# Conditioning weights on a queue and in slots of their own, summed in four stages

## The reference, cut to what matters

```python
for i in range(DEPTH):
    mp = (silu(c_ctx) @ ada_w[i] + ada_b[i]).reshape(6, D_MODEL)      # for the context tokens
    ms = (silu(c) @ ada_w[i] + ada_b[i]).reshape(-1, 6, 1, D_MODEL)   # for the latent tokens
    hp = xp * (1.0 + mp[1]) + mp[0]
    yp = mixer(hp)
    xp = layer_norm(ALPHA * xp + mp[2] * yp)
    ...                                  # the experts with mp[3], mp[4], mp[5]; ms and xs likewise
```

## Time and profile before

| | |
|---|---|
| median of 3 runs | 1439.43 us (1434.58 to 1440.46) |
| the profiled execution | 1439.15 us, of it 1437.3 in the profile's span |
| busy: TensorE, VectorE, ScalarE, GpSimd | 1223.1, 722.3, 344.1, 163.6 us |
| moved by DMA | 290.2 MB, 202 GB/s on average |
| loads of a column, 80 x 512 KB | median 4.7 us from issue to landing, all on SyncE's queue |
| mean granted clock of TensorE | 0.926 |

### The profile page before, as it was taken

The page is one execution under the profiler, slowest core; times in us unless marked ns, Lnnn a source line. Parts: engine busy times, 40 slices in busy tenths (PEclk is TensorE's granted clock), DMA queues, the critical chain, the costliest instruction groups (busy, mean ns, idle before and its releaser), DMA issues.

```text
span 1437.3 us, 14663 instructions
## 1 busy us (share of the span) xinstructions
PE 1223.1 (85%) x5174; PEld 660.0 (46%) x5174; DVE 722.3 (50%) x1580; ACT 344.1 (24%) x728; POOL 163.6 (11%) x222
## 2 busy tenths in 40 slices
PE   6888796999999778999585999989999968899584
PEld 3544354554466333654232555656666423644221
DVE  0598435442312499551013376468886887541114
ACT  1321231222310100311013332234554200311112
POOL 5000310000000000010401401013232000001201
PEclk9999897999999979899798999999999979899797
DMA  9445100327343399189946332234425879199944
GB/s 375 175 162 177 61 1 17 115 105 260 136 167 124 142 335 370 46 356 423 421 204 212 132 125 76 90 112 147 147 85 190 293 275 396 57 400 423 420 169 155
DMA packets 75844, 290.17 MB, mean 202 GB/s; under 512 B 7692, under 2 KB 18188, under 8 KB 61436
## 3 DMA queue, kind: packets, MB, share of 16 engines
q1 hardware_dynamic: 53904, 236.21, 43.3%
q10 hardware_dynamic: 17468, 37.67, 7.4%
q0 software_dynamic: 4400, 15.35, 2.9%
HBM read 261.30 MB, written 27.90 MB: 201 GB/s over the span
## 4 chain that ended last, share of the span: by engine, by line
PE 59%; DVE 13%; DMA 12%; issue 10%; ACT 4%; SPq 1%; ACTq 0%; POOL 0%; POOLq 0%; DVEq 0%
PE bank L580 16%; PE bank L738 7%; PE bank L600 7%; DMA arena<-in_moe_gu 4%; PE bank L947 4%; PE bank L1134 3%; PE bank L758 3%; DVE hT L1884 3%; DVE arena L1908 3%; DMA ring<-in_b_w_out 2%; DMA ring<-in_a_w_down 2%; DVE arena L1884 2%; DVE arena L2460 2%; PE bank L838 2%; PE bank L880 1%
## 5 line engine op out<-in xcount | busy, mean ns | idle before, releaser
L580 PE MATMUL bank<-hT,ring 128*128 128x384 f32 x896 | 304.3, 500 | 18.8 <-DMA ring<-in_a_w_in 14.6
L580 PEld LDWEIGHTS bank<-hT,ring 128*128 128x128 f32 x896 | 173.1, 196 | 142.4 <-issue 19.0
L600 PE MATMUL bank<-ring,arena 128*128 128x512 f32 (+1 forms) x512 | 182.9, 623 | 46.0 <-DMA ring<-in_b_w_out 22.1
L1884 DVE SCALAR_TENSOR_TENSOR hT<-ring,hT 128x1024 f32<-128x1024 f32 x120 | 146.9, 1224 | 9.3 <-DMA ring<-in_ada_wT 5.5
L600 PEld LDWEIGHTS bank<-ring,arena 128*128 128x128 f32 (+1 forms) x512 | 73.5, 198 | 145.9 <-issue 90.9
L738 PE MATMUL bank<-arena,hT 128*64 128x512 f32 x416 | 107.1, 635 | 34.0 <-DMA arena<-in_moe_gu 22.6
L1908 DVE SCALAR_TENSOR_TENSOR arena<-arena,par 128x388 f32<-128x388 f32 x160 | 99.8, 624 | 5.7
L1134 PE MATMUL bank<-hT,ring 128*128 128x384 f32 x256 | 97.6, 507 | 0.2 <-ACT arena L1513 0.2
L738 PEld LDWEIGHTS bank<-arena,hT 128*64 128x64 f32 x416 | 37.5, 146 | 92.1 <-issue 86.4
L2276 DVE TENSOR_TENSOR arena<-arena,bank 128x256 f32<-128x256 f32 x16 | 6.7, 421 | 127.0 <-ACT arena L1635 127.0
L1448 POOL TENSOR_TENSOR arena<-arena 128x192 f32<-128x192 f32 x64 | 43.3, 707 | 214.9 <-PE bank L1167 156.4
(11 more groups left out here) (416 smaller groups left out, 1617.5 us busy)
## 6 DMA issues: line engine op xcount, KB each, us to landing
arena<-in_moe_gu SPq DMA_DIRECT2D x56, 1024.0 KB, 13.3
ring<-in_ada_wT SPq DMA_DIRECT2D x80, 512.0 KB, 4.7
arena<-in_moe_dn SPq DMA_DIRECT2D x28, 1024.0 KB, 19.6
ring<-in_b_w_in SPq DMA_DIRECT2D x40, 512.0 KB, 3.6
ring<-in_a_w_in SPq DMA_DIRECT2D x32, 512.0 KB, 3.5
ring<-in_moe_gu SPq DMA_DIRECT2D x12, 1024.0 KB, 14.2
arena<-acs_rows ACTq DMA_DIRECT2D x32, 384.0 KB, 3.6
yg<-arena ACTq DMA_DIRECT2D x18, 512.0 KB, 7.9
```

Source lines behind the costliest of these rows:

```text
L580: last = mm(keys[j][1][:, 0:T], w[:, k, P * j:P * j + P], hT[:, 4 * half + k, :], start=half == 0 and k == 0, stop=half == 1 and k == 3, s ...
L600: last = mm(keys[t][1][p:p + tokens.shape[1], :], tokens, w[:, j, :], start=k == 0, stop=k == KE - 1, skip_group_check=True)
L1884: ins = ve.scalar_tensor_tensor(out=products, in0=slot(at), scalar=1.0, in1=rows[:, v, :], op0=ALU.mult, op1=ALU.mult, accum_out=mod[:, l, ...
```

## The change

The columns leave `slabs` and the ring. GpSimd issues them on its own queue, in a new function `columns(place)`: it loads the c rows, then the columns one by one into three slots, each as soon as the sum of the column three before is done. Slots, c rows and products lie in parts of the arena that are free in that stage: for places 0 and 1 all six pieces of 1024 together, for 2 and 3 two slots in the scan's old output and one slot and the c rows in `hT`. There are four places with 12, 20, 24 and 24 columns:

- place 0: 12 columns in the first input projection, one after each convolution c = 1 to 12;
- place 1, new: 20 columns in the z projection, two after each gated chunk c = 0 to 9; GpSimd first waits for the end of the scan and of its state outputs;
- place 2: 24 columns in the down projection, where there were 28; GpSimd waits for the last turned-back chunk;
- place 3: 24 columns in the out projection, six between the diagonals and 18 after `rms`; GpSimd waits for its own last products and for the end of the z projection.

SyncE no longer waits for the c rows, nor for sums behind the columns; new is a wait at layer 0's seventh expert slab for 32 sums, since its place overlaps place 1.

```diff
+        c_rows = [v3(a, 2) for a in (free(q_at, 2 * D), free(far_at + 4 * D, 2 * D), hT_free[:, 0:2 * D], hT_free[:, 0:2 * D])]
+        c_slots = [[free(o + D * i) for i in range(3)] for o in (q_at + 3 * D, far_at)]
+        c_slots += [[free(gone_at), free(gone_at + D), hT_free[:, 2 * D:3 * D]]] * 2
+        COLUMNS = (12, 20, 24, 24)
...
         for i in range(2 * KD):
             add("xu", a_in, i // 2, (i % 2,))
-            if i == 1:
-                c_rows_at.append(len(slabs))
-            if i in (1, 2, 4, 5, 7, 8, 10, 11, 13, 14):
-                add_columns(2)
...
                 slabs.append(("down", a_dn[s // 4, 2 * (s % 4) + kp]))
-                if s < 6:
-                    add_columns(4 if (s, kp) in ((1, 0), (2, 1)) else 2)
...
             slabs.append(("out", b_dn[s // 8, s % 8]))
-            if s < 12:
-                add_columns(4 if s in (1, 3, 5, 7) else 2)
...
+                elif l == 0 and m == 6:
+                    sp.wait_ge(sem("summed"), sum(COLUMNS[0:2]))
...
             pool.wait_ge(sem("small_in"), SMALL)
+            def columns(place):
+
+                first = sum(COLUMNS[0:place])
+                pool.wait_ge(sem("small_in"), SMALL + 16 * place)
+                pool.dma_start(c_rows[place].rearrange("p v k -> p (v k)"),
+                               i_["c_rows"].to_broadcast([P, 2 * D])).then_inc(sem("small_in"), 16)
+                for i in range(first, first + COLUMNS[place]):
+                    _, l, j = column_of[i]
+                    if i >= 3:
+                        pool.wait_ge(sem("summed"), i - 2)
+                    pool.dma_start(c_slots[place][i % 3], i_["ada_wT"][l, j]).then_inc(column_landed(i)[0], 16)
+
+            columns(0)
...
+            pool.wait_ge(filled, group["scan_done", 0])
+            for s in range(2):
+                pool.wait_ge(sem(f"out{s}"), 16 * OUT_C)
+            columns(1)
+            pool.wait_ge(filled, group["hn", KE - 1][1])
+            columns(2)
             moe(0)
...
+            pool.wait_ge(sem("xdt_ready"), 2 * KE)
+            pool.wait_ge(sem("wx_ready"), 2 * G)
+            pool.wait_ge(filled, group["in", 3 * KE - 1][1])
+            columns(3)
             moe(1)
...
-                if c in (1, 2, 4, 5, 7, 8, 10, 11, 13, 14):
-                    summed(0, 2)
-            biased(0, 16, 36)
+                if 1 <= c < 13:
+                    summed(0, 1)
+            biased(0, 16, 28)
...
                 ve.tensor_tensor(out=xc, in0=xc, in1=a_sz[:, c, :], op=ALU.mult).then_inc(sem("gA_ready"), 1)
+                if c < 10:
+                    summed(1, 2)
+            biased(0, 28, 48)
...
             diagonals(0)
-            summed(1, 28)
+            summed(2, 24)
...
-            summed(2, 8)
-            biased(1, 16, 24)
...
             diagonals(2, (0, 1))
-            summed(2, 6)
+            summed(3, 6)
             diagonals(2, (2, 3))
...
-            summed(2, 18)
+            summed(3, 18)
             biased(1, 24, 48)
```

67 lines of the change are left out of this document (27 added, 40 removed).

## The result

The changed kernel takes 1429.75 us (median of 20 runs, 1424.68 to 1434.62) against 1438.62 (1431.42 to 1443.68) for the kernel before: a ratio of 0.9941, 95% interval 0.9924 to 0.9957. So it is faster by 8.9 us, where 38.7 were forecast and 1387 to 1424 was the range. The profiled execution has a span of 1431.3 us for 1437.3. Its lines are those of the changed kernel: the sum is L1895, the end of a bias L1904, a convolution's first step L1916, the gating L2084, a projection into the mixer L570, a projection back L590.

The account below looks back on a forecast made before the run. The prediction took the in-order six-slot ring, blocked by columns awaiting VectorE's sums, and waits for VectorE itself as the bound, seldom bandwidth. 23.9 - 2 + 12.8 + 4.0 = 38.7 us off 1439.15 gave 1400, range 1387 to 1424.

Parts of the forecast that it names:

- The first projection: First input projection: fewer columns shorten VectorE's stage by 26.9 us, the start costs 3 (bounds 0 and 6); net 23.9.
- a first k copy later than 132: End of the first input projection: sign that its term is wrong; VectorE's first k copy was expected near 129.
- The z projection: Layer 0: twenty columns come here, VectorE falls back some 7 us and TensorE stalls for banks; 2 us lost.
- The down projection: Layer 0's projection back: 24 columns instead of 28 and a free ring; gain 12.8 us, bounds 16.2 and -23.
- under half of what the engines move: Down projection: SyncE's 2 MB of slabs per 10.4 us until about 532, used to choose a 6 us landing.
- L: Time from a column's issue to landing: 6 then 4.3 us taken in the down projection, 8 in the out projection.
- T: Period per column with three slots, (L + 2.53 + 0.1) / 3: 2.85 us in the down projection, 3.5 in the out.
- The out projection: Layer 1's projection back: 24 columns instead of 32, 18 after the restart as before; gain 4.0 us, bounds 9.2 and -19.
- They move along with the gain: After the projections: the experts' own loads start when routing is planned, so they shift with the gain; 0 us.
- Rival (2): Columns somewhat late throughout, in z, down and out projections; total gain 21.1 us, 1418 us; chance 0.18.
- Rival (3): Three slots cannot cover the queue's latency in the three late stages; slower, 1456 or 1485 us; chance 0.07.
- Rival (4): Projections stay blocked, TensorE now waiting for VectorE through ScalarE's evictions; 1430 to 1440 us; chance 0.04.

Follow-up runs that it names:

- late_start: Changed kernel, but GpSimd's queue issues the c rows and first three columns only once the last ada_w slab has landed; 1422.27 us, 0.9878 of the kernel before.
- z_spread: Changed kernel, with the z projection's 20 columns summed two behind each of the first four chunks, one behind the other twelve; 1432.51 us, 0.9969 of the kernel before.
- experts_held: Changed kernel, with expert slabs moved behind both back projections' slabs and held until the layer's last column sum; 1408.48 us, 0.9791 of the kernel before.
- experts_after: Changed kernel, with expert slabs issued behind the last slabs of the two back projections instead of between them; 1433.65 us, 0.9966 of the kernel before.
- sums_tuned: Changed kernel plus late_start, silu_last and experts_held, with columns also summed in VectorE's idle time in both back projections; 1372.78 us, 0.9530 of the kernel before.
- silu_last: Changed kernel, with ScalarE's SiLU over the last place's c rows behind layer 1's last two state copies; 1423.42 us, 0.9891 of the kernel before.
- late_silu: Changed kernel with late_start and silu_last together; 1420.98 us, 0.9863 of the kernel before.
- five_slots: Changed kernel, with five column slots instead of three in both back projections and three expert slabs held until the last sum; 1408.69 us, 0.9784 of the kernel before.

## Why the prediction was wrong

*What bounds the kernel.* The reading held: slots that waited for VectorE blocked the ring, and with the columns out of it TensorE never waits for a ring slab in the first projection. The forecast that VectorE would still be its bound held too.

*The first projection, 23.9 forecast, 17.4 measured.* The mechanism was right, two terms were mis-sized. The start was put at 3 us of 0 to 6, "half of it lies ahead of slabs that TensorE needs"; it was 7.0 at VectorE, outside the bounds, and late_start gives 6.4 of it back. The half was a guess. The earlier trace rows showed full engines (411 GB/s), and late_start shows that there all of the 2.6 MB issued ahead of the last ada slab were paid, not half. VectorE's stage took 80.9 us for 78.3: chunk and column came every 5.50 us as forecast, but it waited 1.88 us for its second pair of chunks, and the rest are small gaps. The prediction's own sign, a first k copy later than 132, came true (135.64).

*The z projection, -2 forecast, -4.1 measured.* Right in kind: TensorE stalled for VectorE's banks, 2.58 and 1.90 us (the fence under z_spread), behind a VectorE that itself waited 3.1 us for columns, which were not in the sum.

*The down projection, 12.8 forecast, 4.3 measured.* Here the step that failed is "under half of what the engines move". It counted SyncE's 2 MB per 10.4 us, which the profile confirms (2.1 MB per 10.3), and set them against 411 GB/s. It left out the columns' own bytes: 0.52 MB per 2.53 us is 207 GB/s more, together 411. The engines were bound to be full exactly when VectorE ran at its own pace; 495 to 500 us shows 412 GB/s, and from 500 to 530, with VectorE held back, 291 to 383. So L was no property of the queue that could be read from a quiet row: without the expert slabs it is 3.8 to 4.4 (experts_held). The 6 us taken for it was measured at 6.5 to 6.7 (medians, 480 to 532 us), and that alone would give T = 3.1 and cost some 2.5 us more. The sums were 8.0 us longer in all than the 64.2 of the forecast (72.2), because a median is the wrong L for the rule T = (L + 2.63) / 3. Landings differ from column to column, and the longest of each three, 6.7 to 8.0 us, holds up the next round: the four rounds of three columns from 488.95 to 530.76 took 9.5 to 10.9 us each, 3.5 a column for the 2.85 forecast. Where all landings were about equal the rule held: 3.7 for 3.78 (experts_after).

*The out projection, 4.0 forecast, -5.8 measured.* The same omission, with a second one. I had the expert slabs come one by one, while SyncE waits for the last gated chunk until 1127.85 and then lets go 11 issues in 6 us. L was 8.3 to 8.5 us (forecast 8), but for the columns up to 1184 us, 42 us behind the restart, and not for five of them; T was 3.30 over all 18. The SiLU ahead of the state copies cost 2.4 us more of wait (0.56 to 3.00 us; 2.8 had been forecast, and 1.1 to be saved), with a slow clock beside it, but this wait lies in the step before, and so the out projection's own step missed by more than the 9.8 us of the table.

*What lies between.* "They move along with the gain" was wrong by 4.5 and 1.3 us. Of the 4.5 us, 2.4 are the wait for ScalarE just named, and 3.2 lie between VectorE's last part of the down projection and the first expert matmul (28.2 us before, 31.4 after); the rest of the way, some 480 us, is 1.1 us shorter. In the 22 us behind the down projection the clock stood at 0.66 (574 to 596 us), against 0.70 in the kernel before (592 to 614). TensorE's 21.92 us of idle time is not the reason: sums_tuned, with 1.23 us idle there, has 0.65 in the same step. late_start, silu_last and late_silu, with the same program there, need 29.8 us, so half of the 3.2 us does not recur; the cause of the rest stays open, and no run here varied it alone.

*The rivals.* Rival (2), columns somewhat late throughout, with L = 7 and T = 3.2, was the right one in mechanism and gave 1418. With 4.0 more at the start and the 5.8 us between, that is 1428, near the profiled 1433. In part that is luck: it had -0.9 for the out projection, which lost 5.8, and it had already counted the wait for ScalarE that is among the 5.8 us between. Rival (3) had the right kind of bound. Taken for one projection at a time, its terms turn at T = 3.3 in the down projection (69.3 - 21 T) and at 3.14 in the out projection (47.1 - 15 T); the sums took 3.0 and 3.3 us each, and one projection back gained 4.3 and the other lost 5.8. Rival (4) falls: it would have shown TensorE waiting through the first projection. In experts_held columns land in 3.8 and 4.4 us with VectorE busy 59.7 of 64 us. By the Trainium skill (SBUF — State Buffer, Who interferes with whom) GpSimd cannot write descriptors while VectorE holds the shared port, but an operation with two inputs, as this sum is, takes only its read side; the page marks that as inferred. The trace agrees with the exception, not with a price of 1.2 us: GpSimd issued every column in 0.53 us beside the sums. The Trainium skill's fit for one DMA (DMA: Bandwidth & Descriptors, Anatomy of one DMA; an estimated 3.2 us) lies 0.6 to 1.2 us below the same rows and far below the 6.5 to 8.5 of full engines.

*The range* ended at 1424 because L was drawn from single rows of a queue. The bytes asked for would have moved both projections back to the slow side at once, and rival (2) would have been the forecast.

## What to carry to other kernels

Before taking a landing time from a quiet row, add up all the bytes that will be asked for per unit of time once the consumer runs at its own pace, those of the moved transfers too; at the engines' limit the landing time is an outcome, and the number of slots has a say in who gets the bandwidth. With few slots, go by the longest landing of a round, not by the median. A shared in-order queue that looks like an obstacle may also be the priority rule that keeps urgent transfers ahead of idle-time ones, so whoever takes transfers out of it must hold the others back in another way. And when the bound of a stage is one engine's work, first look for that engine's own idle time in the same stage: filling it brought 21.7 us here, about as much as the best of the repairs.

## What the runs showed of the hardware that I had not expected

- As far as these rows go, two queues share full DMA engines by what each has in flight. In layer 1's out projection three slots of 512 KB let GpSimd issue a column every 3.82 us, 137 of 409 GB/s (the changed kernel, 1156 to 1183 us), and five slots every 2.74 us, 191 of 413 GB/s (five_slots, 1131 to 1159), though each column then took up to 13.0 us to land.
- A 512 KB load on GpSimd's queue lands in 3.8 to 4.4 us (medians) while VectorE is busy over 90% (experts_held), no slower than the same load on SyncE's queue in the kernel before (median 4.7).
- TensorE's granted clock fell around the last state matmuls of layer 1 in most kernels: over 8 us to a mean of 0.50 to 0.57 in six of the seven kernels where TensorE waited 2.4 us or more there, and to 0.79 or not at all in the others; eight matmuls took 2.04 to 2.08 us there for 1.16.
